# Expert-choice top-k of a hybrid DeltaNet/Hyena layer: sample halves and prompt side by side on 48 partitions, merged by one comparison

## The reference

```python
def expert_choice_ffn(u, w_router, w_gate, w_up, w_down):
    bsz, l, _ = u.shape
    cap = EC_FACTOR * l // N_EXPERTS
    probs = jax.nn.softmax((u @ w_router).astype(jnp.float32), axis=-1)
    aff, idx = lax.top_k(jnp.swapaxes(probs, 1, 2), cap)
    bidx = jnp.arange(bsz)[:, None, None]
    xs = u[bidx, idx]
    hid = jax.nn.silu(jnp.einsum('becd,edf->becf', xs, w_gate)) * jnp.einsum('becd,edf->becf', xs, w_up)
    ys = jnp.einsum('becf,efd->becd', hid, w_down) * aff[..., None].astype(u.dtype)
    return jnp.zeros_like(u).at[bidx, idx].add(ys)
```

## Time and profile before

| what | value |
|---|---|
| median of 3 runs | 1540.01 us (1539.88 to 1544.6) |
| the profiled execution's own time | 1536.6 us |
| its span in the profile | 1534.7 us |
| busy: PE, PEld, DVE, ACT, POOL | 1414.4, 762.0, 475.3, 239.7, 71.2 us |
| mean granted clock of TensorE | 0.975 |
| HBM read, written | 283.95 MB, 17.30 MB |

### The profile page before, as it was taken

One profiled execution on the slowest core, in us unless ns is written; L12 is line 12 of the kernel. 1 busy time (PEld: TensorE's weight loads), 2 busy tenths in 40 slices (PEclk: granted clock), 3 DMA queues, 4 the chain that ended last, 5 costly groups with the idle time before them and its releaser, 6 DMA issues.

```text
span 1534.7 us, 24351 instructions
## 1 busy us (share of the span) xinstructions
PE 1414.4 (92%) x10826; PEld 762.0 (50%) x10826; DVE 475.3 (31%) x1079; ACT 239.7 (16%) x463; POOL 71.2 (5%) x63
## 2 busy tenths in 40 slices
PE   4999999998999999999999972999999999999991
PEld 1455554555988885555555431344444443433430
DVE  3412224335566761102102667111111111111115
ACT  3211121313333322100000013000001000000010
POOL 0000000000000000000000000011111111111110
PEclk9999999999999999999999996999999999999996
DMA  9911324312000000423012135799999999999984
GB/s 367 347 66 55 113 106 165 110 55 69 3 2 2 3 3 14 164 110 123 0 56 93 70 146 216 279 360 384 391 393 392 393 393 384 385 393 393 393 335 147
DMA packets 91915, 302.19 MB, mean 197 GB/s; under 512 B 3419, under 2 KB 7515, under 8 KB 90956
## 3 DMA queue, kind: packets, MB, share of 16 engines
q1 hardware_dynamic: 80764, 274.19, 46.4%
q0 software_dynamic: 7680, 17.11, 4.4%
q10 hardware_dynamic: 3408, 9.96, 1.7%
HBM read 283.95 MB, written 17.30 MB: 196 GB/s over the span
## 4 chain that ended last, share of the span: by engine, by line
PE 49%; DMA 14%; DVE 4%; issue 1%; ACT 0%; SPq 0%; POOL 0%; DVEq 0%; POOLq 0%
PE bank L516 48%; DMA ring<-w_e_up_dram 14%; DVE hbuf L1632 1%; DVE misc L1681 0%; DVE front L1486 0%; DVE hbuf L1755 0%; DVE misc L1679 0%; DVE stats L1753 0%; DVE front L1682 0%; PE bank L851 0%; PE bank L544 0%; PE bank L886 0%; DMA front<-u_dram,misc 0%; DMA y_dram<-front,misc 0%; PE bank L457 0%
## 5 line engine op out<-in xcount | busy, mean ns | idle before, releaser
L516 PE MATMUL bank<-front,ring 128*128 128x512 f32 x1768 | 501.3, 444 | 0.9 <-ACT front L934 0.9
L516 PE MATMUL bank<-ring,front 128*32 128x256 f32 (+2 forms) x3296 | 435.6, 462 | 6.5 <-DMA ring<-w_e_up_dram 4.3
L516 PEld LDWEIGHTS bank<-front,ring 128*128 128x128 f32 x1768 | 272.7, 191 | 232.2 <-issue 229.7
L516 PEld LDWEIGHTS bank<-ring,front 128*32 128x32 f32 (+2 forms) x3296 | 175.0, 124 | 265.0 <-issue 214.8
L516 PE MATMUL bank<-front 128*32 128x256 f32 (+3 forms) x2976 | 272.8, 352 | 4.4 <-DVE front L1546 2.4
L516 PEld LDWEIGHTS bank<-front 128*32 128x32 f32 (+3 forms) x2976 | 164.0, 139 | 107.3 <-issue 81.8
L1735 DVE TENSOR_TENSOR front<-bank,front 128x512 f32<-128x512 f32 x16 | 11.1, 692 | 281.0 <-PE bank L516 281.0
L1321 DVE SCALAR_TENSOR_TENSOR front<-bank,pk,front 128x511 f32<-128x511 f32 x64 | 32.2, 545 | 110.2 <-ACT front L954 109.7
L1486 DVE COPY_PREDICATED front<-ck,bank 128x256 f32<-128x256 uint32 (+1 forms) x120 | 52.8, 444 | 24.0 <-PE bank L516 21.7
L1147 ACT ACTIVATE front<-bank 128x512 f32<-128x512 f32 x16 | 9.6, 597 | 279.6 <-PE bank L516 279.6
L516 PE MATMUL bank<-front,misc 64*64 64x64 f32 (+1 forms) x912 | 44.6, 237 | 5.2 <-ACT misc L1069 5.2
(11 more groups left out here) (237 smaller groups left out, 896.6 us busy)
## 6 DMA issues: line engine op xcount, KB each, us to landing
ring<-w_e_gate_dram SPq DMA_DIRECT2D x32, 2048.0 KB, 19.3
ring<-w_e_up_dram SPq DMA_DIRECT2D x32, 2048.0 KB, 20.2
front<-w_e_down_dram SPq DMA_DIRECT2D x32, 2048.0 KB, 19.8
ring<-w_in_dram SPq DMA_DIRECT2D x11, 2048.0 KB, 9.1
ring<-w_mod_dram SPq DMA_DIRECT2D x10, 2048.0 KB, 11.5
front<-w_mod_dram SPq DMA_DIRECT2D x2, 2048.0 KB, 19.6
ring<-const_dft_f_dram SPq DMA_DIRECT2D x2, 2048.0 KB, 13.6
ring<-w_out_dram SPq DMA_DIRECT2D x2, 2048.0 KB, 7.8
```

The lines of the kernel that those rows point to most:

```text
L516: return pe.matmul(out, lhsT, rhs, start=(k == 0), stop=(k == n - 1))
```

## The change

The sample's 512 columns are split in two halves of 256. The two halves and the prompt lie side by side on 48 partitions: partitions 0 to 15 hold tokens 0 to 255 of each expert, 16 to 31 tokens 256 to 511, 32 to 47 the prompt's 128 tokens with -1 behind them. Eight rounds run on all 48 partitions at once and give 64 values and indices in falling order on each; of the prompt's the first 16 are used. Values and indices (cast to floats) are transposed, and two products bring the second half's list, reversed by a constant matrix `flip`, and the prompt's list to partitions 0 to 15. With one list falling and the other rising, the greater of each pair is one of the best 64 of both, so one comparison merges them: a step of 0 or 1 selects between token and token of the second half + 256.

The probabilities are multiplied into `halved` (tiles 0, 2, 4 and tiles 1, 3 next to each other), so that two transposes do for five. The table `ck` grows by 128 columns in its first part. `top_value`, `top_token` and two new lists move to other columns of `misc`.

```diff
-for _name, _n in (("ident", P), ("ones", P), ("eps", 4), ("offset", NT), ...
+for _name, _n in (("ident", P), ("ones", P), ("eps", 4), ("flip", P), ("offset", NT), ...
+    put("flip", (i[:, None] // HB == i[None, :] // HB) & (i[:, None] % HB + i[None, :] % HB == HB - 1))
...
-        rrow = reg(EW + 2048, TOK)[0:16, :]
+        HALF = SEQ_S // 2
+        rrow = reg(EW + 2048, HALF)[0:3 * E, :]
+        halved = dec[:, 80:160]
-        top_value = misc[0:16, 640:720]
-        top_index = misc[0:16, 720:800].bitcast(U32)
-        top_token = misc[0:16, 800:880]
+        top_list = misc[0:3 * E, 640:768]
+        top_index = misc[0:3 * E, 768:832].bitcast(U32)
+        top_value = misc[0:16, 2240:2320]
+        top_token = misc[0:16, 2320:2400]
+        list_T = misc[:, 2400:2448]
...
-            pe.wait_ge(sem("probs"), 1)
-            for t in range(NT):
-                i = pe.transpose(bank[6 + t // 4][0:16, P * (t % 4):P * (t % 4) + P], probs[:, t, 0:E], ident)
-            i.then_inc(sem("prob_tr"), 1)
+            pe.wait_ge(sem("probs"), 2)
+            pe.transpose(bank[6][0:3 * E, 0:P], halved[:, 0:3 * E], ident)
+            pe.transpose(bank[6][0:2 * E, P:2 * P], halved[:, 3 * E:5 * E], ident).then_inc(sem("prob_tr"), 1)
+            pe.wait_ge(sem("top_list"), 1)
+            pe.transpose(bank[7][:, 0:3 * E], top_list, ident[0:3 * E, 0:3 * E]).then_inc(sem("list_tr"), 1)
+            pe.wait_ge(sem("list_T"), 1)
+            mm(bank[5][0:E, 0:P], list_T[:, E:2 * E], C("flip"))
+            mm(bank[5][0:E, P:2 * P], list_T[:, 2 * E:3 * E], ident).then_inc(sem("list_back"), 1)
...
-            V.tensor_tensor(probs[:, :, 0:E], probs[:, :, 0:E], rsum.unsqueeze(2).to_broadcast([P, NT, E]), ALU.mult) \
-                .then_inc(sem("probs"), 1)
+            for j, a, n in ((0, 0, 3), (1, 3 * E, 2)):
+                V.tensor_tensor(halved[:, a:a + n * E].rearrange("p (t e) -> p t e", t=n), probs[:, j::2, 0:E],
+                                rsum[:, j::2].unsqueeze(2).to_broadcast([P, n, E]), ALU.mult).then_inc(sem("probs"), 1)
             s = Stage("topk")
+            s.add(V.memset(rrow[2 * E:3 * E, SEQ_C:HALF], -1.0))
             dve.wait_ge(sem("prob_tr"), 1)
-            s.add(V.tensor_copy(rrow[:, 0:SEQ_S], bank[6][0:16, :]))
-            s.add(V.tensor_copy(rrow[:, SEQ_S:TOK], bank[7][0:16, 0:SEQ_C]))
-            s.settle()
-            for a, l, at, rounds in ((0, SEQ_S, 0, CAP_S // 8), (SEQ_S, SEQ_C, CAP_S, CAP_C // 8)):
-                row = rrow[:, a:a + l]
-                for r in range(rounds):
-                    eight = slice(at + 8 * r, at + 8 * r + 8)
-                    s.add(V.max(top_value[:, eight], row))
-                    s.settle()
-                    s.add(V.max_index(top_index[:, eight], top_value[:, eight], row))
-                    s.add(V.match_replace(row, top_value[:, eight], row, -1.0))
-                    s.settle()
-            s.add(V.tensor_copy(top_token[:, 0:CAP_S], top_index[:, 0:CAP_S]))
-            s.add(V.tensor_copy(top_token[:, CAP_S:CAP], top_index[:, CAP_S:CAP]))
-            s.settle()
-            s.add(V.tensor_scalar(top_token[:, CAP_S:CAP], top_token[:, CAP_S:CAP], float(SEQ_S), None, ALU.add))
+            s.add(V.tensor_copy(rrow[:, 0:SEQ_C], bank[6][0:3 * E, 0:SEQ_C]))
+            s.add(V.tensor_copy(rrow[0:2 * E, SEQ_C:HALF], bank[6][0:2 * E, SEQ_C:HALF]))
+            s.settle()
+            for r in range(CAP_S // 8):
+                eight = slice(8 * r, 8 * r + 8)
+                s.add(V.max(top_list[:, eight], rrow))
+                s.settle()
+                s.add(V.max_index(top_index[:, eight], top_list[:, eight], rrow))
+                s.add(V.match_replace(rrow, top_list[:, eight], rrow, -1.0))
+                s.settle()
+            V.tensor_copy(top_list[:, CAP_S:2 * CAP_S], top_index).then_inc(sem("top_list"), 1)
+            dve.wait_ge(sem("list_tr"), 1)
+            V.tensor_copy(list_T, bank[7][:, 0:3 * E]).then_inc(sem("list_T"), 1)
+            dve.wait_ge(sem("list_back"), 1)
+            value, token = top_list[0:E, 0:CAP_S], top_list[0:E, CAP_S:2 * CAP_S]
+            value_2, token_2 = bank[5][0:E, 0:CAP_S], bank[5][0:E, CAP_S:2 * CAP_S]
+            step = lane_aff[:, 1, 0:CAP_S]
+            s.add(V.tensor_tensor(step, value_2, value, ALU.is_gt))
+            s.add(V.scalar_tensor_tensor(top_token[:, 0:CAP_S], token_2, float(HALF), token, ALU.add, ALU.subtract))
+            s.add(V.tensor_tensor(top_value[:, 0:CAP_S], value_2, value, ALU.max))
+            s.add(V.tensor_copy(top_value[:, CAP_S:CAP], bank[5][0:E, P:P + CAP_C]))
+            s.add(V.tensor_scalar(top_token[:, CAP_S:CAP], bank[5][0:E, P + CAP_S:P + CAP_S + CAP_C], float(SEQ_S), None, ALU.add))
+            s.settle()
+            s.add(V.tensor_tensor(top_token[:, 0:CAP_S], top_token[:, 0:CAP_S], step, ALU.mult))
+            s.settle()
+            s.add(V.tensor_tensor(top_token[:, 0:CAP_S], top_token[:, 0:CAP_S], token, ALU.add))
             s.settle()
```

More of the change, by code:

```diff
@@ L67 @@
 _at = 0
-for _name, _n in (("ident", P), ("ones", P), ("eps", 4), ("offset", NT), ("lane_row", P), ("first_row", P), ("tri_f", P), ("tri_b", P),
+for _name, _n in (("ident", P), ("ones", P), ("eps", 4), ("flip", P), ("offset", NT), ("lane_row", P), ("first_row", P), ("tri_f", P), ("tri_b", P),
                   ("neg_f", P), ("neg_b", P), ("ident_half", HB), ("masks", (LEVELS - 1) * 3 * HB), ("spare", 320)):
```

## The result

| | before | changed |
|---|---|---|
| median | 1538.83 us | 1531.86 us |
| lowest to highest | 1534.35 to 1545.12 us | 1527.17 to 1536.73 us |
| the profiled execution, its span | 1536.6, 1534.7 us | 1532.17, 1530.3 us |

The kernel before was timed again with the changed one, 20 runs each; its median moved from 1540.01 to 1538.83 us. The ratio of the times is **0.9952, 95% interval 0.9940 to 0.9964**: 7.4 us faster, between 5.5 and 9.2 us. Forecast were 6.7 us and 1533.3 us; of the 1.4 us between 1533.3 and 1531.86, 1.2 us are the kernel before, whose own median moved. The page shows little of it: the clock's 25th slice is at 7 tenths in place of 6, and the shares of the last chain have moved little (TensorE 49 to 51%, DMA 14 to 13%).

What follows compares the result with a forecast made beforehand. VectorE's top-k was taken to bound the stretch before expert 0, with the weight stream's start tied to it. -8.30 - 0.40 - 0.33 + 2.1 + 0.2 = -6.7 us, from 1540.0 to 1533.3 us; range 1529.5 to 1537.5 us.

Steps and rivals of the forecast that it cites:

- The bound: Before expert 0, VectorE's top-k alone sets the pace; the weight stream's start is tied to it, so the whole saving reaches the end.
- expert 1's gate load near 968.6 us: Sign in the changed profile: SyncE issues expert 1's gate weights near 968.6 us, at 975.31 us before.
- Rival (b): Weight stream of the last eight experts takes back 3 us; no measurable change, within 0.3%, 1536.3 or 1538 us; chance 0.16.
- The rounds: VectorE's top-k: ten rounds taking 19.14 us become eight of 1.355 us, 10.84 us in all; 8.30 us saved.
- rival (c): Top-k operations cost by element, partitions times columns: 2.96 us a round, 6.1 us slower in all, 1546.1 us; chance 0.03.
- Copies and probability transposes: Ahead of the top-k: shorter copies into rrow save 0.40 us, two probability transposes for five save 0.33 us.
- the two products: After the rounds, TensorE's two list products with 128 moving columns at the low clock: 0.69 us added.
- merge: VectorE's merging of the two lists after the products, five independent operations, then multiply, add and a signal: 1.15 us.
- the bound of 3.4: Upper bound on the 2.1 us added after the rounds, if each of four hand-offs costs 0.34 us more.
- PSUM or the Trainium skill's price: Merge's PSUM reads: rows say little added; the skill's count says 65 ns for each of five operations, sum 0.3 us slower.
- The table: Constant table's first part, loaded at the start, grows by 64 KB: 0.2 us added, between 0 and 0.35 us.
- Rival (a): Added transposes and products bring TensorE's clock back sooner at expert 0: up to 1.8 us more gain, 1531.5 us; chance 0.05.

Runs made afterwards that it cites:

- twice: The changed kernel with the eight top-k rounds run twice, first on a copy of the rows; 1.0036 of the kernel before's time.
- warm: The changed kernel with 18 unread 512-column products added on TensorE, in groups of 11, 5 and 2; 0.9954 of the kernel before's time.
- direct: The changed kernel with identity-slice products bringing the lists down, without list transpose, copy or flip; VectorE reads one backwards; 0.9948 of the kernel before's time.

## Why the prediction was right

**The bound.** VectorE's top-k was on the one chain, and the weight stream did begin with expert 0. Shown two ways: by twice (10.97 us more ahead of expert 0, the same 571.8 us behind it) and by the kernel before and the changed one, the other way (572.1, 571.7 and 571.8, 571.0, 571.6). The sign that the forecast named, expert 1's gate load near 968.6 us, came at 971.04, less the 2.34 us of the late start 968.7. Rival (b) expected 3 us to be taken back; none is, within the scatter of 1.5 us.

**The rounds.** -8.30 us forecast, 10.89 - 19.14 = -8.25 measured. The line between 128 and 512 columns held: by the groups of the DVE lines, MAX8 420 ns (0.42 forecast), FIND_INDEX8 409 ns, MATCH_REPLACE8 401 ns.

```profile
L1688 DVE MAX8 misc<-front 48x8 f32<-48x256 f32 x8 | 3.4, 420 | 0.3
L1690 DVE FIND_INDEX8 misc<-misc,front 48x8 uint32<-48x256 f32 x8 | 3.3, 409 | 0.0
...
L1691 DVE MATCH_REPLACE8 front<-misc,front 48x256 f32<-48x256 f32 x8 | 3.2, 401 | 0.0
```

With 48 partitions they are on the line of 16, so rival (c), a price by the element, is refuted: it gave 2.96 us a round, and a round takes 1.36.

**Copies and probability transposes.** -0.73 forecast; the first probability transpose to the first MAX8 goes from 1.65 to 0.93 us (933.01 - 931.36, 934.62 - 933.69), -0.72.

**The step that was mis-sized** is the two products: "0.45 + 0.22 + 0.02 = 0.69 us". They take 1.07 us to VectorE's next start. I counted a product as one matmul. In fp32, the type of these operands, one is two here: the trace has four for the two, 0.45 + 3 x 0.22 = 1.1 us, and the earlier trace rows had it already, where the gate's spread is 32 matmuls for the code's 16 products. A transpose is one, which is why the other terms fit: transpose 0.35 + 0.02 (0.32 forecast), copy 0.22 + 0.04 (0.25), cast 0.20 + 0.04 (0.23), merge 948.65 - 947.46 = 1.19 (1.15). The sum is 3.14 instead of 2.64 us, inside the bound of 3.4 plus 0.53.

**PSUM or the Trainium skill's price.** An operation on two operands costs the same with one of them in PSUM (L1700) as with both in SBUF (L1706):

```profile
947.46 0.21 DVE L1700 TENSOR_TENSOR misc<-bank,misc 16x64 f32<-16x64 f32 x1 [1.13 <-PE bank L521]
...
948.13 0.21 DVE L1706 TENSOR_TENSOR misc<-misc 16x64 f32<-16x64 f32 x1
```

The merge took 1.19 us, 1.15 by the rows. The Trainium skill ("VectorE: DVE Perf Modes", the section on the TRN2 errata) counts 62 cycles more for a PSUM source, by which I had put each such operation at 65 ns more; no such difference is in these lines, and by it the merge would have been near 1.5 us. That the whole sum so raised, 2.96 us, lies nearer to the 3.14 measured than my 2.64 is luck: what was missing were the products, not PSUM. The Trainium skill's bf16 latency of a single matmul ("TensorE: Matmul & The Clock Gate", single matmul latency), which the prediction set beside its own row, would have made the miss on the products larger.

**The table** could not be measured: 0.2 us against a start that scatters by over 1 us.

**The clock.** Rival (a) in its own form did not happen: the added transposes and products did not bring the clock back (0.50 from 945 to 950 and at 958.6 us). Its price, put at up to 1.8 us, was 1.6 to 2.8 us once products were added that did: 12.5 to 13.7 less 10.9 us.

**The sum.** -8.25 - 0.72 + 2.61 = -6.4 us by the steps of the traces, -6.7 forecast, -7.0 between the medians, -5.5 to -9.2 by the interval of the ratio. The 0.5 us that the hand-offs cost more are not seen in the times: the medians' 7.0 us lie as far above the forecast as the steps' 6.4 us below it, and both distances are smaller than the interval. That the forecast is hit to 0.3 us is in part luck.

## What to carry to other kernels

Serial work on one engine with narrow tiles is shortened by folding its columns onto idle partitions: halving the columns halves all of an operation but a fixed 0.15 us, and the added partitions cost nothing; the price is the way back, here 2.6 us, in which each step between engines is the operation's own length plus 0.02 to 0.04 us. (Shown here for MAX8, FIND_INDEX8 and MATCH_REPLACE8, from 128 to 512 columns and for 16 and 48 partitions.) Here the stream of loads starts with the work behind such a stage, and the saving reaches the end whole, to within the scatter of 1.5 us, although the loads set the pace of the late experts. Compare two profiles from a mark on, not by their spans: here the spans hid a third of the gain behind a clock that falls in other places from one profile to the next.

## What was not expected of the hardware

- The granted clock goes with the scatter. The kernel before had spans of 1534.7 and 1541.2 us. By the same instructions the second profile was 0.56 us ahead at 59 us and 6.43 us behind at 452 us; between them the clock stood at 0.65 instead of 0.86 over 25 us. Of its runs on that chip, those over 1542 us have a mean clock of 0.967 or 0.968, those under 1537 us 0.973 to 0.975.
- A waiting TensorE was not free: 1.6 to 2.8 us at the start of the experts. Products that nobody reads took it off, but they paid only where they were over, or nearly so, when the real work arrived; ten matmuls too late cost about as much as the clock gave (warm).
- VectorE reads PSUM backwards at the price of forwards (0.21 and 0.20 us for 16x64, direct), and a slice of the identity moves rows between partitions in one product (two matmuls), with no transpose on either side.
